# Latent attention issued by half heads, with two score tiles of the next head and two turns of this one in turn

## The reference, cut to what matters

```
def attend(blk):
    qn, qr = blk
    s = (jnp.einsum('bqhd,bkhd->bhqk', qn, k_nope)
         + jnp.einsum('bqhr,bkr->bhqk', qr, k_rope))
    p = jax.nn.softmax(s.astype(jnp.float32) * scale, axis=-1).astype(v.dtype)
    return jnp.einsum('bhqk,bkhd->bqhd', p, v)
```

## Time and profile before

| | before |
|---|---|
| median of three runs | 3110.86 us |
| the profiled execution | 3109.12 us |
| its span | 3107.3 us |
| TensorE busy | 3023.5 us (97%) |
| VectorE busy | 1702.9 us (55%) |
| ScalarE busy | 1182.1 us (38%) |
| GpSimd busy | 1235.6 us (40%) |
| granted TensorE clock, mean | 0.989 |

### The profile page before, as it was taken

How to read it: one execution, slowest core, us unless ns; L and a number is a source line. 1 busy time by engine, 2 the same in 40 slices (tenths; PEclk the granted TensorE clock), 3 DMA queues, 4 the chain that set the end, 5 groups by cost and what they waited for, 6 DMA issues and landing times.

```text
span 3107.3 us, 41472 instructions
## 1 busy us (share of the span) xinstructions
PE 3023.5 (97%) x16448; PEld 2534.3 (82%) x16448; DVE 1702.9 (55%) x2822; ACT 1182.1 (38%) x1826; POOL 1235.6 (40%) x584
## 2 busy tenths in 40 slices
PE   8999999999999999999999999999999999999999
PEld 7658888886589888778888998878888789878887
DVE  4545676845463553655328866676684457442113
ACT  4643212235445333234336645532223335332222
POOL 4314444533266333333444554444444330244442
PEclk9999999999999999999999999999999999999999
DMA  8214554622245223223333333345653220123331
GB/s 132 65 50 124 166 162 137 182 65 65 70 129 151 83 72 92 82 68 106 112 102 99 113 113 107 128 132 180 190 157 114 76 68 2 41 72 102 99 95 68
DMA packets 480433, 323.87 MB, mean 104 GB/s; under 512 B 102520, under 2 KB 447744, under 8 KB 479728
## 3 DMA queue, kind: packets, MB, share of 16 engines
q1 hardware_dynamic: 475472, 309.60, 34.0%
q10 hardware_dynamic: 2656, 6.30, 0.5%
q0 software_dynamic: 2112, 5.32, 0.5%
HBM read 315.90 MB, written 5.24 MB: 103 GB/s over the span
## 4 chain that ended last, share of the span: by engine, by line
PE 89%; DVE 6%; ACT 2%; issue 1%; POOL 1%; DMA 0%; DVEq 0%; ACTq 0%; POOLq 0%
PE G L2949 13%; PE G L2958 13%; PE G L2959 12%; PE G L2963 12%; PE G L3178 6%; PE G L3179 6%; PE G L3183 6%; PE G L2976 3%; PE G L4097 1%; PE G L3748 1%; PE SS L3306 1%; PE G L3410 1%; PE G L3343 1%; PE SS L2949 1%; POOL WL L757 1%
## 5 line engine op out<-in xcount | busy, mean ns | idle before, releaser
L757 POOL TENSOR_TENSOR WL<-raw,WH 128x1024 fp32r<-128x1024 f32 (+1 forms) x520 | 1192.6, 2316 | 1747.6 <-ACT WH L828 1747.5
L828 ACT ACTIVATE WH<-raw 128x1024 fp32r<-128x1024 f32 (+1 forms) x520 | 492.6, 995 | 596.4 <-PE G L3183 404.2
L2958 PE MATMUL G<-hH,WH 128*128 128x512 f32 x1520 | 595.1, 391 | 0.7 <-ACT xtok L1562 0.7
L2959 PE MATMUL G<-hL,WH 128*128 128x512 f32 x1520 | 591.9, 389 | 0.0
L2963 PE MATMUL G<-hH,WL 128*128 128x512 f32 x1520 | 359.9, 389 | 0.0
L2958 PEld LDWEIGHTS G<-hH,WH 128*128 128x128 f32 x1520 | 285.4, 188 | 61.4 <-ACT xtok L1562 0.9
L2963 PEld LDWEIGHTS G<-hH,WL 128*128 128x128 f32 x1520 | 285.3, 188 | 59.2
L2959 PEld LDWEIGHTS G<-hL,WH 128*128 128x128 f32 x1520 | 285.4, 188 | 58.5
L1758 DVE SCALAR_TENSOR_TENSOR acc<-adaw,cvec,acc 128x512 f32<-128x512 f32 x280 | 280.1, 1053 | 4.2
L1782 DVE TENSOR_TENSOR FH<-silu,G 128x512 fp32r<-128x512 f32 x44 | 30.3, 688 | 245.4 <-PE G L2963 191.0
L2949 PE MATMUL G<-hH,WH 128*128 128x512 f32 (+1 forms) x416 | 161.5, 388 | 0.0
(11 more groups left out here) (825 smaller groups left out, 6040.3 us busy)
## 6 DMA issues: line engine op xcount, KB each, us to landing
raw<-ffn_w_in_in SPq DMA_DIRECT2D x264, 256.0 KB, 3.4
adaw<-ada_w_in SPq DMA_DIRECT2D x48, 1024.0 KB, 5.3
raw<-ab_w_in_in SPq DMA_DIRECT2D x128, 256.0 KB, 3.0
raw<-ffn_w_out_in SPq DMA_DIRECT2D x96, 256.0 KB, 3.0
raw<-w_gate_in SPq DMA_DIRECT2D x88, 256.0 KB, 3.3
raw<-w_up_in SPq DMA_DIRECT2D x88, 256.0 KB, 3.4
raw<-w_down_in SPq DMA_DIRECT2D x64, 256.0 KB, 3.0
raw<-w_in_in SPq DMA_DIRECT2D x40, 256.0 KB, 3.3
```

The lines of the kernel that those rows point to most:

```text
L757: nc.gpsimd.tensor_tensor(WL[c % 2][:, cut], raw[c % 2][:, cut], WH[c % 2][:, cut].bitcast(F32), ALU.subtract)\
L828: nc.scalar.activation(WH[c % 2][:, cut], raw[c % 2][:, cut], ACT.Copy).then_inc(weights_hi, 1)
L2958: mm(dst, view(WH[c % 2], k), high, start=(k == 0 and not (joint and i)), stop=False)
L2959: mm(dst, view(WH[c % 2], k), low, start=False, stop=False)
```

## The change

The two halves of a head are now issued in turn on all three engines. TensorE issues scores 0 and 1 of head h+1, a half of a pair's values, turns 0 and 1 of head h, scores 2 and 3 of head h+1, turns 2 and 3 of head h. A score tile now waits for the exponential of its own bank and not for that of the fourth tile. ScalarE goes through evictions 0 and 1 and exponentials 0 and 1, then 2 and 3 of each; the high part of a pair stands at the beginning of a head, and the conversion of chunk c+4 behind head 2 instead of head 1. VectorE takes one maximum of the next head and one scaling in turn, and writes the shared keys one head earlier than they are used. Token values 2 and 3 are computed in heads 0 and 1 and both go through G[3] (table VALUES).

```diff
+        VALUES = (G[0], G[1], G[3], G[3])
...
                 for k in range(4):
                     exponents(k)
-                    if k % 2:
-                        token_values(k // 2)
+                token_values(0)
+                token_values(1)
                 for h in range(NH):
-                    for i in range(4):
-                        spread(n, 4 * h + i)
-                    if h + 1 < NH:
-                        for i in range(4):
-                            exponents(4 * h + 4 + i)
-                            if h == 0 and i >= 2:
-                                token_values(i)
-                    if h % 2 == 0 and h:
+                    if h < 2:
+                        token_values(2 + h)
+                    elif h % 2:
                         high_out(n, h // 2 - 1)
-                    if h == 1:
+                    for half in range(2):
+                        for i in range(2 * half, 2 * half + 2):
+                            spread(n, 4 * h + i)
+                        if h + 1 < NH:
+                            for i in range(2 * half, 2 * half + 2):
+                                exponents(4 * h + 4 + i)
+                    if h == 2:
                         hi(c + 4)
...
+                largest(0)
+                largest(1)
+                for i in range(2):
+                    largest(2 + i)
+                    scaled(n, i)
                 for h in range(NH):
-                    largest(4 * h)
-                    largest(4 * h + 1)
-                    if 1 < h + 1 < NH:
-                        shared_keys(h + 1)
-                    for i in range(2, 4):
-                        scaled(n, 4 * h + i - 2)
-                        largest(4 * h + i)
-                    for i in range(2, 4):
-                        scaled(n, 4 * h + i)
+                    for i in range(2):
+                        if h + 1 < NH:
+                            largest(4 * h + 4 + i)
+                        scaled(n, 4 * h + 2 + i)
+                    if h + 2 < NH:
+                        shared_keys(h + 2)
                     if h % 2 and h > 1:
                         low_out(n, h // 2 - 1)
+                    if h + 1 < NH:
+                        for i in range(2):
+                            largest(4 * h + 6 + i)
+                            scaled(n, 4 * h + 4 + i)
...
-                def scores(h):
-                    pe.wait_ge(act_done, at("act", f"{n}.kn{h}"))
-                    pe.wait_ge(dve_done, at("dve", f"{n}.kr{h}"))
-                    if h:
-                        pe.wait_ge(act_done, at("act", f"{n}.exp{4 * h - 1}"))
-                    for i in range(4):
+                def scores(h, tiles):
+                    if tiles[0] == 0:
+                        pe.wait_ge(act_done, at("act", f"{n}.kn{h}"))
+                        pe.wait_ge(dve_done, at("dve", f"{n}.kr{h}"))
+                    for i in tiles:
+                        if h:
+                            pe.wait_ge(act_done, at("act", f"{n}.exp{4 * h - 4 + i}"))
...
                 for h in range(NH):
-                    for i in range(4):
-                        turn_probs(n, 4 * h + i)
-                    if h + 1 < NH:
-                        scores(h + 1)
-                    if h == 0:
-                        token_values(2)
-                        token_values(3)
-                        tally.also("pe", f"used.{c}")
-                    elif h % 2 and h + 1 < NH:
-                        values(n, h // 2, range(2))
-                    elif h % 2 == 0:
-                        values(n, h // 2 - 1, range(2, 4))
+                    for tiles in (range(2), range(2, 4)):
+                        if h + 1 < NH:
+                            scores(h + 1, tiles)
+                        if tiles[0] == 0:
+                            if h < 2:
+                                token_values(2 + h)
+                                if h == 1:
+                                    tally.also("pe", f"used.{c}")
+                            elif h % 2 == 0:
+                                values(n, h // 2 - 1, range(2))
+                            else:
+                                values(n, h // 2 - 1, range(2, 4))
+                        for i in tiles:
+                            turn_probs(n, 4 * h + i)
...
-                elif s == 4:
-                    pe.wait_ge(act_done, at("act", f"{n}.vt2"))
-                elif s:
+                else:
                     pe.wait_ge(act_done, at("act", f"{n}.ptA{s - 3 if i == 3 else s - 4 if i else s - 1}"))
```

More of the change, by code:

```diff
@@ L1015, in token_values @@
                     act.wait_ge(pe_done, at("pe", f"{n}.vt{k}"))
-                    nc.scalar.activation(vtok[:, k, :], G[k][:, :], ACT.Copy).then_inc(act_done, did("act", f"{n}.vt{k}"))
+                    nc.scalar.activation(vtok[:, k, :], VALUES[k][:, :], ACT.Copy).then_inc(act_done, did("act", f"{n}.vt{k}"))
                 for k in range(4):
                     exponents(k)
-                    if k % 2:
-                        token_values(k // 2)
+                token_values(0)
+                token_values(1)
                 for h in range(NH):
-                    for i in range(4):
-                        spread(n, 4 * h + i)
-                    if h + 1 < NH:
-                        for i in range(4):
-                            exponents(4 * h + 4 + i)
-                            if h == 0 and i >= 2:
-                                token_values(i)
-                    if h % 2 == 0 and h:
-                        high_out(n, h // 2 - 1)
-                    if h == 1:
+                    if h < 2:
+                        token_values(2 + h)
+                    elif h % 2:
+                        high_out(n, h // 2 - 1)
+                    for half in range(2):
[5 more added lines that the diff above has]
+                    if h == 2:
                         hi(c + 4)
@@ L3298, in first_mixing @@
                         .then_inc(pe_done, did("pe", f"{n}.kh{h}"))
-                def scores(h):
-                    pe.wait_ge(act_done, at("act", f"{n}.kn{h}"))
-                    pe.wait_ge(dve_done, at("dve", f"{n}.kr{h}"))
-                    if h:
-                        pe.wait_ge(act_done, at("act", f"{n}.exp{4 * h - 1}"))
-                    for i in range(4):
+                def scores(h, tiles):
[5 more added lines that the diff above has]
+                            pe.wait_ge(act_done, at("act", f"{n}.exp{4 * h - 4 + i}"))
                         mm(SCORES[i][:, :], qT[:, h, i * P:i * P + P], kT[:, h, :], start=True, stop=True).then_inc(pe_done, did("pe", f"{n}.sc{4 * h + i}"))
-                    if h == NH - 1:
+                    if h == NH - 1 and tiles[-1] == 3:
                         tally.also("pe", f"{n}.att.scores")
                 pe.wait_ge(dve_done, at("dve", f"{n}.mL7"))
-                scores(0)
+                scores(0, range(4))
                 def token_values(k):
-                    pe.wait_ge(act_done, at("act", f"{n}.kn{(2 * k + 2) % NH + 1}"))
-                    if k == 2:
-                        pe.wait_ge(act_done, at("act", f"{n}.ptA3"))
+                    pe.wait_ge(act_done, at("act", f"{n}.kn{(3, 5, 1)[k]}" if k < 3 else f"{n}.vt2"))
                     cut = bass.ds(k * P, P)
-                    three(G[k][:, :], 2, lambda q: (ckH[:, q, cut], ckL[:, q, cut]), weights_of(c, lambda w, q: heads(w, 1, q)))\
+                    three(VALUES[k][:, :], 2, lambda q: (ckH[:, q, cut], ckL[:, q, cut]), weights_of(c, lambda w, q: heads(w, 1, q)))\
                         .then_inc(pe_done, did("pe", f"{n}.vt{k}"))
@@ L3390, in turn_probs @@
                 pe.wait_ge(dve_done, at("dve", f"{n}.pn{s}"))
-                if s in (1, 2):
+                if s == 0:
+                    pe.wait_ge(act_done, at("act", f"{n}.kn7"))
+                elif s in (1, 2):
                     pe.wait_ge(act_done, at("act", f"{n}.vt{i - 1}"))
-                elif s == 4:
-                    pe.wait_ge(act_done, at("act", f"{n}.vt2"))
-                elif s:
+                else:
                     pe.wait_ge(act_done, at("act", f"{n}.ptA{s - 3 if i == 3 else s - 4 if i else s - 1}"))
@@ L3406, in values @@
                         pe.wait_ge(dve_done, at("dve", f"{n}.aL{pair - 1}"))
+                    else:
+                        pe.wait_ge(act_done, at("act", f"{n}.vt3"))
                 for k in ks:
```

## The result

The changed kernel took 3090.4 us, the median of four executions (3088.52 to 3094.61), beside 3111.91 for the kernel before; the ratio is 0.9935 with a 95% interval of 0.9922 to 0.9948. The before of this comparison, 3111.91 us, is the median of four executions too. Two later comparisons (e1 and e11) gave 0.9953 (0.9940 to 0.9966) and 0.9951 (0.9934 to 0.9967), 15 us. The profiled execution, the slowest of the four, took 3094.61 us with a span of 3092.8: 14.5 us under the profiled execution of the kernel before.

A forecast was written before the change was run, and what follows sets the result against it. The prediction took the hand-off ring of TensorE, ScalarE and VectorE to bound the attentions. Of waits of 8.1 and 8.3 us, block 0 saves 5.9 and block 1 6.5, together 12.4: 3096.7, beside the median 3098.4; range 3092 to 3106.

The forecast's parts named there:

- TensorE becomes the bound, all three hand-offs hide: Ring of TensorE, ScalarE and VectorE in half heads: TensorE stops waiting and binds, shortest reserve 0.7 us.
- the reserve of 0.7 us in odd and 1.1 in even heads: Banks of scores 0 and 1: free at 6.2 us (6.6 in odd heads), needed at 7.3.
- A head of 7.36 us: TensorE's steady head in the new order: scores, values, turns and two switches, against 8.04 to 9.76 before.
- The second switch from scores: TensorE's extra change from scores to other work in each head: 0.09 us, 0.6 us a block.
- The GpSimd collision at 1.2 us a block: GpSimd's two subtractions hold tile 3's scaling and the shared keys, so scores wait: 1.2 us, between 0 and 3.5.
- 0.37 us kept at the end: Head 7: turn 3 waits for eviction 0 behind the high part, at 3.64 instead of 3.27 us.
- The context's wait falls from 1.03 to 0.65: Block 1, behind the last turns: the context's transposes wait 0.65 us for their DMA instead of 1.03.
- The conversion hidden behind head 2: ScalarE's weight chunk conversion runs from 9.4 to 11.4 us, before its next work is due at 11.5.
- Start: First heads of each attention: head 0's wait for its third turn disappears; nothing more taken, between -0.3 and +0.6 us.
- the lower end of the range: Kernel time of 3092 us: the best end, 3094.6, with the spread of the runs.
- All waits together are 17.4 us, and no reordering of the same instructions gets more: TensorE's waits in both attentions and before the context's transposes: 17.4 us as the most any reordering could gain.

The follow-up runs named there:

- e1: The changed kernel unchanged, measured again against the kernel before: 3093.26 us, ratio 0.9953.
- e11: The changed kernel unchanged, measured a third time: 3096.28 us, ratio 0.9951.
- e9: The changed kernel with two more ScalarE copies of 128x512 a head, output unused: 3099.26 us in one execution.
- e10: The changed kernel with two more VectorE reductions of 64x512 a head, behind the scalings of tiles 2 and 3: 3110.21 us in one execution.
- e3: The changed kernel with the weight chunk's conversion moved from head 2 to behind the last eviction: 3100.74 us, ratio 0.9976.
- e6: As e3, with the context DMA ahead of that chunk's subtraction in GpSimd's queue of block 1: 3087.64 us, ratio 0.9916.
- e4: The kernel before, with only the weight chunk's conversion moved behind the last eviction, no half heads: 3117.41 us, ratio 1.0027.
- e12: The same kernel as e6, measured again beside e11: 3090.0 us, ratio 0.9934.

## Why the prediction was wrong in size and right in mechanism

- *TensorE becomes the bound, all three hand-offs hide.* Right: no steady head waits. e9 and e10 find ScalarE's exponentials and VectorE's sum of work as the next bounds, within about 1 us a head; the reserve of 0.7 us in odd and 1.1 in even heads was not found as such.
- *A head of 7.36 us* was mis-sized, and this is the largest error of the sum: 7.20 to 7.21. The second switch from scores costs nothing (765.41 to 767.13 is 1.72 for two tiles before the turns; only the step to the values has 0.09), and the turns take 1.80 and not 1.87 (0.93 and 0.87). Over seven heads that is 1.1 us a block.
- *The GpSimd collision at 1.2 us a block*: 1.25 by starts (8.45 against 7.20), through the keys, and both held operations end with a subtraction, as predicted, 2.30 and 2.47 us against the 2.62 of the earlier trace rows. Without it block 0 is 1.33 us shorter (e3 and e6).
- *0.37 us kept at the end*: the sixteen turns of the last head run through in 1.93 us (186.08 to 188.01 in block 0), 0.05 over the 1.88 of four times 0.47. The prediction let the values end at 2.3 us, though they start at 0 and take 1.87. In block 1 they end at 800.10; the high part starts 0.12 behind that, eviction 0 at 800.79, and a turn can follow an eviction's start by 0.75 (816.30 to 817.05 before): 801.54, when TensorE, at 0.47 a tile, has done the three turns ahead of it (801.51).

```profile
800.22 0.60 ACT L1234 ACTIVATE hH<-G 128x512 fp32r<-128x512 f32 x1
800.79 2.06 ACT L1228 ACTIVATE pt<-G 128x512 f32<-128x512 f32 x4
```
```profile
800.10 2.07 PE L3408 MATMUL G<-ident,pm 128*128 128x128 f32 x16
```

- *The context's wait falls from 1.03 to 0.65*: it did not fall. Reckoned by starts in the same way it is 803.09 - 800.10 - 1.93 = 1.06. (The profile's brackets say 0.87 before and 0.92, 0.84 and 0.69 in the three profiles of the changed kernel.) The turns ended 0.3 earlier than predicted, the DMA did not.
- *The conversion hidden behind head 2*: right, ScalarE's evictions started at 772.43 and 774.97, 0.6 to 0.8 us behind the starts of their turns (771.68 and 774.33). That it must not move further, since GpSimd's queue carries the context DMA behind it, I hadn't seen; the change didn't need it, e3 and e4 did.
- *Start*: no wait up to head 3, as said.

These terms explain 2.9 us: together the attentions gave 15.3 us where I had 12.4. The other 5.1 of the 8.0 us between 3098.4 and 3090.4 lie outside the attentions, which I had put at no change. The runs show no gain there: from the profile before to the one after the start and the middle change by under 0.1 us and the tail is 1.0 longer, and e1 and e11 measured 15 us. They show one kernel's medians 5.9 us apart (3090.40, 3093.26, 3096.28) and stretches at the lower clock that come and go. So the excess of the first comparison is put down to spread, and the two later medians, which lie in the range, are as much the luck of a sample as the first.

The step that failed is thus the lower end of the range. "All waits together are 17.4 us, and no reordering of the same instructions gets more" bounded the gain by the waits of one profile, with the spread of three executions set beside it. That bound was too low in two ways. The waits were too few, since the work was counted too high, by turns of 0.47 and a switch a head: e6 and e12 got 8.9 us out of block 0, where the prediction counted 8.1. And with start and tail each moving by 5 to 8 us from execution to execution, the median of four executions could fall further from the profiled one than I allowed; 1.6 us more would have covered it.

## What to carry to other kernels

Where three engines hand one tile set round a ring, lay one period on paper with the hand-off times of the trace. Here every engine's sum of work was under the old period, and halving the unit and waiting by bank brought the period down to the sum of the busiest engine, 7.20 us. Halving alone isn't enough: with the wait left on the whole unit the same order was 11 to 12 us an attention slower than before. And cut the profiles at named instructions before comparing them: the attentions repeat to 0.2 us where medians of one kernel lie 6 us apart. Before moving an operation, look at what stands behind its consumer in a third engine's queue (here a DMA on GpSimd).

## What the runs showed of the hardware that I had not expected

A wait of 2.17 us on TensorE was followed in some heads by scores at half the rate (3.65 us instead of 1.96 for two tiles) and in others not, in one and the same stretch; the granted clock over the 4 us from 154 was 0.57, over those from 165 it was 1.00. And the stretches at the lower clock (1.2 GHz) move from execution to execution: between the attentions they took 0.0, 1.7, 3.4 or 5.1 us in 14 profiles, in no relation to the change, and two profiles of one kernel differ by 7.6 us behind the attentions. A VectorE scaling or key operation held by a subtraction of GpSimd ended 0.3 us behind that subtraction, and VectorE's held operation came in between the two subtractions: each of the two operations was held for one subtraction only.
